# All up rows of the first token tile gathered and summed within the second tail

## What is computed

```python
h = rms_norm(x, g[0]) * (1.0 + scale1) + shift1
y = hybrid_mixer(h, positions, w_in[l], ...)      # attention and convolution, gates, w_out
x = x + gate1 * rms_norm(y, g[1])
h = rms_norm(x, g[2]) * (1.0 + scale2) + shift2
q = (h @ w_q)...; s1, s2 = scores against sub_keys; top 16 of each, top 16 of the sums -> expert, gate
def chunk(args):
    xc, ic, gc = args
    pre = jnp.einsum('td,tkd->tk', xc, expert_down[ic])
    act = jax.nn.gelu(pre, approximate=False) * gc
    return jnp.einsum('tk,tkd->td', act, expert_up[ic])
x = x + gate2 * rms_norm(y, g[3])
```

## Time and profile before

| | |
|---|---|
| median of three runs | 4313.49 us |
| profiled execution | 4317.19 us, span 4315.4 us, granted clock 0.752 |
| TensorE busy | 2814.7 us, 65% |
| VectorE busy | 2301.3 us, 53% |
| GpSimd busy | 1443.1 us, 33% |
| moved by DMA | 1413.21 MB, mean 327 GB/s |
| chain that ended last | TensorE 42%, DMA 37%, VectorE 11%, GpSimd 5% |

### The profile page before, as it was taken

How to read it: one execution, slowest core, us unless ns; L and a number is a source line. 1 busy time by engine, 2 the same in 40 slices (tenths; PEclk the granted TensorE clock), 3 DMA queues, 4 the chain that set the end, 5 groups by cost and what they waited for, 6 DMA issues and landing times.

```text
span 4315.4 us, 37435 instructions
## 1 busy us (share of the span) xinstructions
PE 2814.7 (65%) x15012; PEld 1619.7 (38%) x15012; DVE 2301.3 (53%) x3585; ACT 541.6 (13%) x1191; POOL 1443.1 (33%) x1109
## 2 busy tenths in 40 slices
PE   3797899977899999997893334434344334434435
PEld 2686787877875555453451101101001001101101
DVE  7397697652176233325465555664555664444442
ACT  2211211210110000111111101100001001000000
POOL 2321212000003223233233356454356454354352
PEclk9898999988999999998995555555555555555555
DMA  7544424488658889889688899999999999999998
GB/s 287 183 173 149 139 99 163 171 328 316 201 198 342 305 347 367 344 336 366 253 322 335 355 404 422 412 413 422 416 399 412 412 412 422 421 422 422 421 421 370
DMA packets 303724, 1413.21 MB, mean 327 GB/s; under 512 B 24384, under 2 KB 24512, under 8 KB 167104
## 3 DMA queue, kind: packets, MB, share of 16 engines
q0 software_dynamic: 152064, 1107.36, 62.6%
q1 hardware_dynamic: 145568, 291.53, 19.4%
q10 hardware_dynamic: 5920, 11.94, 0.7%
HBM read 1403.35 MB, written 7.39 MB: 327 GB/s over the span
## 4 chain that ended last, share of the span: by engine, by line
PE 42%; DMA 37%; DVE 11%; POOL 5%; issue 4%; ACT 2%; SPq 0%; ACTq 0%; DVEq 0%; POOLq 0%
PE psum L610 42%; DMA front<-in_down,back 22%; DMA front<-in_up,back 9%; POOL front L581 4%; DVE front L1577 3%; DMA front<-in_w_in 2%; DMA back<-in_ada_w 2%; DVE back L1290 1%; DVE back L1352 1%; DMA back<-in_up,back 1%; ACT back L1116 1%; DVE back L1555 0%; POOL back L581 0%; DVE back L1512 0%; DVE back L1521 0%
## 5 line engine op out<-in xcount | busy, mean ns | idle before, releaser
L610 PE MATMUL psum<-front 128*32 128x512 f32 (+2 forms) x6608 | 1410.0, 664 | 999.2 <-DMA front<-in_up,back 851.8
L1577 DVE CUSTOM_DVE_ANT_0 front<-front,back 128x2048 f32<-128x2048 f32 x512 | 1168.7, 2291 | 1391.5 <-DMA front<-in_down,back 1274.4
L610 PEld LDWEIGHTS psum<-front 128*32 128x32 f32 (+1 forms) x6608 | 582.3, 163 | 1759.7 <-issue 1404.6
L581 POOL DMA_INDIRECT front<-in_down,back x512 | 622.1, 1215 | 930.1 <-DVE back L1577 657.6
L581 POOL DMA_INDIRECT front<-in_up,back x442 | 539.5, 1221 | 1001.1 <-PE psum L610 953.8
L610 PE MATMUL psum<-back,front 128*32 128x128 f32 (+3 forms) x4400 | 636.0, 457 | 331.9 <-DMA back<-in_up,back 164.2
L610 PEld LDWEIGHTS psum<-back,front 128*32 128x32 f32 (+1 forms) x4400 | 372.2, 168 | 603.1 <-issue 316.6
L559 POOL TENSOR_TENSOR w_low<-front,w_high 128x2048 fp32r<-128x2048 f32 x33 | 153.4, 4650 | 589.5 <-ACT w_high L1004 589.5
L610 PE MATMUL psum<-x_high,w_high 128*128 128x512 f32 x640 | 258.6, 404 | 51.1 <-issue 22.4
L610 PE MATMUL psum<-x_low,w_high 128*128 128x512 f32 x640 | 256.1, 400 | 0.0
L610 PE MATMUL psum<-x_high,w_low 128*128 128x512 f32 x640 | 255.9, 400 | 0.0
(11 more groups left out here) (160 smaller groups left out, 1700.5 us busy)
## 6 DMA issues: line engine op xcount, KB each, us to landing
front<-in_w_in SPq DMA_DIRECT2D x116, 1024.0 KB, 6.7
back<-in_ada_w SPq DMA_DIRECT2D x64, 1024.0 KB, 8.5
front<-in_ada_w POOLq DMA_DIRECT2D x32, 1024.0 KB, 8.6
front<-in_w_out SPq DMA_DIRECT2D x32, 1024.0 KB, 5.6
front<-in_w_q SPq DMA_DIRECT2D x32, 1024.0 KB, 5.4
front<-in_w_conv_o SPq DMA_DIRECT2D x16, 1024.0 KB, 6.8
front<-in_w_attn_o SPq DMA_DIRECT2D x16, 512.0 KB, 3.8
front<-in_down,back POOLq DMA_INDIRECT x512
```

What stands on the lines that cost most here:

```text
L581: nc.gpsimd.indirect_dma_start(out=row_, out_offset=None, in_=table[:, :], in_offset=bass.IndirectOffsetOnAxis(ap=idx4[:, t % 2, c:c + 1], ...
L610: return nc.tensor.matmul(o, a, b, start=start, stop=stop)
L1577: V.tensor_tensor_reduce(d_row[s], d_row[s], h2r, 1.0, 0.0, ALU.mult, ALU.add, pre[:, b // 16 % 2, b % 16:b % 16 + 1]).then_inc(dots_done, 1)
```

## The change

Positions are decoupled from blocks. There are 32 more positions (`DRAIN`), and `place(p)` maps a position to a block number and to the range of blocks that is being worked on: up to 160 the first tile's, and behind that block p - 32 of the others. A step is done only where its block lies in the range. So at positions 128 to 159 no down row of the second tile is worked on, while the last up rows of the first are summed; and at positions 160 to 183 there is no up row. GpSimd's queue is cut in the same way. `PACE` now brings all 160 positions into the first 71 chunks of `tail(1)` (up to the first four of w_q), evenly, with 2 or 3 a chunk. Two waits on TensorE are adapted: the fifth h2 turn waits for the fourth `finish`, and `z_sum` of groups 3 and 15 for the h2 turns up to their own group only.

```diff
-END = BLOCKS + 64
+DRAIN = 32
+END = BLOCKS + DRAIN + 64
+
+def place(p):
+    return (p, 0, 128) if p < 128 + DRAIN else (p - DRAIN, 128, BLOCKS)
...
 def block_pace():
-    at, out = 0, []
-    for i in range(tail_chunks(1)):
-        if 64 <= i < 67:
-            at += (3, 3, 2)[i - 64]
-        else:
-            at += 1 + i % 2
-        out.append(at)
-    assert at == 128, at
-    return out
+    last = 48 + 16 + TAIL[1][1] // P + 4
+    return [min((i + 1) * (128 + DRAIN) // last, 128 + DRAIN) for i in range(tail_chunks(1))]
...
-            for i in range(BLOCKS + UP_LAG):
-                if i < BLOCKS:
+            for first, last in ((0, 128), (128, BLOCKS)):
+                for i in range(first, last + UP_LAG):
+                    if i < last:
...
-                b = i - UP_LAG
-                if b >= 0:
+                    b = i - UP_LAG
+                    if b >= first:
...
                 if J >= 2 and i == 0:
-                    pe.wait_ge(out_ready, J - 1)
+                    pe.wait_ge(out_ready, J if J == 4 else J - 1)
...
-                pe.wait_ge(h2r_ready, min(4 * (J + 2), 4 * GROUPS))
+                pe.wait_ge(h2r_ready, 4 * (J + 1) if J in (3, GROUPS - 1) else 4 * (J + 2))
...
-                    p = pos_
-                    if p % 32 == 0 and p < BLOCKS:
+                    b, first, last = place(pos_)
+                    if b % 32 == 0 and b < last:
                         for i in range(4):
-                            h2_quarter(p // 32, i)
-                    if 0 <= p - LAG < BLOCKS:
-                        weighted_rows(p - LAG)
-                    J = p // 32 - 1
-                    if 0 <= J < GROUPS and p % 32 == 25:
+                            h2_quarter(b // 32, i)
+                    if first <= b - LAG < last:
+                        weighted_rows(b - LAG)
+                    J = b // 32 - 1
+                    if first <= 32 * J < last and b % 32 == 25:
                         z_sum(J)
```

More of the change, by code:

```diff
@@ L586, in _ @@
             pool.wait_ge(ada2_used, 2 * KT)
-            for i in range(BLOCKS + UP_LAG):
-                if i < BLOCKS:
[L589 to L596, removed]
-                b = i - UP_LAG
-                if b >= 0:
[L599 to L604, removed]
+            for first, last in ((0, 128), (128, BLOCKS)):
+                for i in range(first, last + UP_LAG):
+                    if i < last:
+                        s, _, prev = D_SLOT[i]
+                        if i % 128 < 32 and i % 8 == 0:
+                            pool.wait_ge(routed, 4 * (i // 128) + i % 128 // 8 + 1)
+                        if prev is not None:
+                            pool.wait_ge(dots_done, prev + 1)
+                        if i == WIDE:
+                            pool.wait_ge(g_done, DONE[1, "sc", 3] + 4)
+                        gather(down, d_row[s], i, d_in[s])
+                    b = i - UP_LAG
+                    if b >= first:
+                        s, _, prev = U_SLOT[b]
+                        if prev is not None:
+                            pool.wait_ge(u_used, prev + 1)
+                        if b == WIDE:
+                            pool.wait_ge(g_done, DONE[1, "sc", 3] + 4)
+                        gather(up, u_row[s], b, u_in[s])
         @block.tensor
@@ L849, in retrieve @@
                 while pos_ < upto:
-                    p = pos_
-                    if p % 32 == 0 and p < BLOCKS:
+                    b, first, last = place(pos_)
+                    if b % 32 == 0 and b < last:
                         for i in range(4):
-                            h2_quarter(p // 32, i)
-                    if 0 <= p - LAG < BLOCKS:
-                        weighted_rows(p - LAG)
-                    J = p // 32 - 1
-                    if 0 <= J < GROUPS and p % 32 == 25:
+                            h2_quarter(b // 32, i)
[3 more added lines that the diff above has]
+                    if first <= 32 * J < last and b % 32 == 25:
                         z_sum(J)
-                    if 0 <= J < GROUPS and p % 32 == 27:
+                    if first <= 32 * J < last and b % 32 == 27:
                         x2_rows(J)
@@ L1144, in retrieve @@
                 while pos_ < upto:
[L1145 to L1155, removed]
+                    b, first, last = place(pos_)
+                    if b % 32 == 0 and b < last:
+                        h2_quarters(b // 32)
+                    unit = b // 16 - 1
+                    if first <= 16 * unit < last:
+                        if b % 16 == 3:
+                            unit_gelu(unit)
+                        if 7 <= b % 16 < 15:
+                            block_weights(16 * unit + 2 * (b % 16 - 7))
+                            block_weights(16 * unit + 2 * (b % 16 - 7) + 1)
+                    J = b // 32 - 1
+                    if first <= 32 * J < last and b % 32 == 24:
                         z_squares(J)
-                    if 0 <= J < GROUPS and p % 32 == 26:
+                    if first <= 32 * J < last and b % 32 == 26:
                         z_std(J)
-                    t, n = p // 128 + 1, (p % 128 - 34) // 24
-                    if t >= 2 and t < TT and p % 128 >= 34 and (p % 128 - 34) % 24 == 0 and n < 4:
+                    t, n = b // 128 + 1, (b % 128 - 34) // 24
+                    if first and t < TT and b % 128 >= 34 and (b % 128 - 34) % 24 == 0 and n < 4:
                         gate_exp(t, n)
@@ L1605, in retrieve @@
                 while pos_ < upto:
-                    p = pos_
-                    J = p // 32 - 1
-                    if 0 <= J < GROUPS and p % 32 == 28:
+                    b, first, last = place(pos_)
+                    J = b // 32 - 1
+                    if first <= 32 * J < last and b % 32 == 28:
                         finish(J)
[L1610 to L1616, removed]
+                    if b < last:
+                        dot(b)
+                    unit = b // 16 - 1
+                    if b % 16 == 5 and first <= 16 * unit < last:
+                        unit_act(unit)
+                    t, n = b // 128 + 1, (b % 128 - 28) // 24
+                    if first and t < TT and b % 128 >= 28 and n < 4:
+                        if (b % 128 - 28) % 24 == 0:
                             route(t, n)
-                        if (p % 128 - 28) % 24 == 12:
+                        if (b % 128 - 28) % 24 == 12:
                             gates(t, n)
```

## The result

The changed kernel takes 4389.18 us (median of four, 4384.42 to 4397.84) against 4314.50 of before beside it: 1.0176 times as long, 95% interval 1.0163 to 1.0189. Forecast were 4350 us, +36.5; it is +75. The direction was right and the time lies in the range, but the size is double. The profiled execution has a span of 4389.4 us against 4315.4, +74.0.

The account below looks back on a forecast made before the run. TensorE was taken to bound the second tail, with DMA nearly full, and DMA the stretch behind. The tail grows by 79.5 us, 43 are gained behind it: 4317.2 + 36.5 - 3.7 = 4350 us, range 4301 to 4393.

Parts of the forecast that it names:

- (a): Chunks 4 to 15 of the second tail: TensorE 132.5, DMA 135.5, taken as 135 us, +21.5.
- (b): Chunks 16 to 51 of the second tail: DMA becomes the bound, 504 us, +78; ends 485 and 520.
- (c): Chunks 52 to 63 of the second tail: 169.5 us, +17, the first five still at the DMA's pace.
- (d): x chunks and first chunks of w_q: no dot product between the residual sums any more, together -15 us.
- (e): Chunks 71 to 82 of the second tail: 18 positions go, and two in the last chunk, -22 us.
- (f): Behind the tail, dot products 128 to 152 without up rows, 3.1 us a step: gain 43 us, ends 35 and 55.
- Faster: Rival: TensorE stays the bound in the tail, which grows by under 43 us; 4289 us, chance 0.19.
- The clock: Rival: the granted clock may not hold in chunks 16 to 51, 0.77 considered; 4370 to 4410 us, chance 0.08.
- The rule of 358 GB/s: HBM loads bound at about 358 GB/s a core: chunks 16 to 51 take 571 us, total 4417, chance 0.02.

Follow-up runs that it names:

- e1: The changed kernel with only the first 12 chunks of the second tail at the old pace (18 positions instead of 27): 4368.69 us, 1.0130 of the kernel before.
- e5: The changed kernel with up gathers of blocks 3 to 127 fetching 4 KB pieces instead of 8 KB rows: 4326.09 us, 1.0026 of the kernel before.
- e2: The changed kernel with its 160 positions spread evenly over all 83 chunks, 1.93 a chunk: 4336.42 us, 1.0056 of the kernel before.
- w2: The changed kernel with five slots for down rows from block 131 and for up rows from block 128: 4362.72 us, 1.0106 of the kernel before.

## Why the prediction was right in direction and half in size

- **(a), the step that failed.** It took the larger of TensorE's and the DMA's sum, 135 us, and was 166.4. It looked at the order of GpSimd's queue and of TensorE's, but never asked what stands behind the added dot products on VectorE: the gate products, for which TensorE waits. That wait, 25.9 us, was in no term of the sum. The trace of before had what it needed: at 3.48 us a dot 20 of them take 70 us, and w_attn_o ends some 46 us after the first one. e1 shows the wait go and 20 us of the 75 with it. The other 5 us are the h2 turn, put at 8 and measured at 13.
- **(b), right, a little low.** DMA became the bound, as forecast: share 0.99, 47.7 us of waits for up rows. 504 us were 513.9: 195 MiB at 399 GB/s, 2.63 us a MiB instead of 2.585. e5 shows the cause, e2 that it goes with the density. The rate stayed under the 422 that the lower bound used. The upper end, 520 with gaps at both h2 turns, had the right mechanism: 317 and 340 GB/s around them, 411 to 413 elsewhere.
- **A misread price.** The sum counts three h2 turns in (b) of the kernel before and gets 8 us for one. Its trace has two there, at 1465 and 1732 us, so the 26 us left over give (26 - 2)/2 = 12 each. With 12, TensorE's sum for (b) is 458 instead of 450, and 459 were measured; since the DMA's was larger, the forecast doesn't change by it, but (a) would have been 136.5.
- **(c) and (d)**: +11.0 for +17, -20.5 for -15. TensorE was busy 161 of 164 us in (c), so the bound had gone back to it. **(e)**: -20.6 for -22, 11.0 us a chunk with its share of score products; the window from 2240 to 2372 us has a DMA share of 0.31.
- **(f), the second size that was off.** Of the bounds 2.52 and 3.48 us the middle was taken, 3.1; it was 3.38, near the measured upper end, which had been discounted for chunk loads beside it. The start of 9 us was 10.0, and the last two steps were already at 4.97, as up gathers begin at block 150. w2 shows what sets it.
- **The rivals.** Faster (TensorE stays the bound) would have needed 438 GB/s; it was 399. The clock: 0.94 in (b), not 0.77. The rule of 358 GB/s of the Trainium skill (DMA: Bandwidth & Descriptors, "Where 436 GB/s comes from") is contradicted again for this one core, by 399 GB/s in mixed traffic and 416 with gathers alone. The warning of the Trainium skill on idle gaps (TensorE: Matmul & The Clock Gate, "Why this matters for your kernels") agrees with the trace where the waits are longest: 0.61 in the 5 us behind the 25.9 us, and 0.50, with h2 parts of 1.94 instead of 1.08 us, behind a wait of 5.05. Over (b), with waits of at most 5.2 us, it comes to no more than 0.94.

What stays open: how long the DMA engines' gap at an h2 turn is and what sets it (40 us at 317 GB/s in one place, at 372 in another), how the 26 us of wait and the work moved out of (a) share the 20 us of e1, and how the 18 to 31 us over both sums in e2 split between TensorE's bursts and the DMA engines' gaps; no run separates them.

## What to carry to other kernels

When work is moved under a stretch that is bound elsewhere, add up the second engine's time there before and after: at a DMA share of 0.88 to 0.94 there is no room for half as much again, and from 1.93 to 2.25 positions a chunk cost 53 us, 10 of them by the first wait. Then walk through each engine's program order and ask which result stands behind the work that was added; a wait appears there that no sum of busy times shows. A moved step can still be worth it once its pace fits and its far end is repaired: the same move, thinly spread and with five slots behind the tail, gave 4289 us.

## What the runs showed of the hardware

An indirect gather of 64 rows of 8 KB into 64 partitions took the DMA engines 3.2 us, one of 128 rows 2.55 us, and one of 128 pieces of 4 KB 1.5 us. Fewer partitions didn't make a gather cheaper; shorter pieces did, though not in proportion. Beside chunk loads the engines were full at 411 to 415 GB/s away from h2 turns, and moved 392 to 404 over stretches that hold them; with gathers alone they moved 416. Down rows alone with three slots came in 3.38 us each, with five in 2.63.
